# Opening loads of a two-block transformer kernel: first weight piece and transposed input in two halves, the other loads issued behind them

## The reference, cut to what matters

```
for l in range(DEPTH):                       # DEPTH = 2
    q, k, v, r, a_low, u, v_sgu = split_proj(x @ w_in[l])
    y_gla = gla_group(q, k, v, r, a_low, w_a2[l], b_a[l], gla_norm_g[l])
    y_sgu = sgu_group(u, v_sgu, w_s[l], b_s[l], sgu_ln_g[l], sgu_ln_b[l])
    h = jnp.concatenate([y_gla, y_sgu], axis=-1) @ w_out[l]
    x = layer_norm(DN_ALPHA * x + h, ...)
    x = layer_norm(DN_ALPHA * x + mem_xattn(x, mem, ...), ...)
    x = layer_norm(DN_ALPHA * x + grouped_moe(x, ...), ...)
...
# second block: its modulation vectors come from c alone
m = jax.nn.silu(c) @ w + b                   # adaln, w is 1024 x 6144, per layer
```

## Time and profile before

| | |
|---|---|
| median of three runs | 2224.72 us (2221.09 to 2226.09) |
| profiled execution, its own time | 2221.31 us |
| its span, first to last instruction | 2219.5 us |
| PE / PEld busy | 2040.2 us (92%) / 1579.8 us (71%) |
| DVE / ACT / POOL busy | 1564.4 us (70%) / 1067.9 us (48%) / 60.2 us (3%) |
| moved by DMA | 574.60 MB, 259 GB/s over the span |

### The profile page before, as it was taken

The page is one execution under the profiler, slowest core; times in us unless marked ns, Lnnn a source line. Parts: engine busy times, 40 slices in busy tenths (PEclk is TensorE's granted clock), DMA queues, the critical chain, the costliest instruction groups (busy, mean ns, idle before and its releaser), DMA issues.

```text
span 2219.5 us, 24051 instructions
## 1 busy us (share of the span) xinstructions
PE 2040.2 (92%) x9132; PEld 1579.8 (71%) x9132; DVE 1564.4 (70%) x1998; ACT 1067.9 (48%) x1090; POOL 60.2 (3%) x86
## 2 busy tenths in 40 slices
PE   7999989999799997999997988799999777899996
PEld 4566578888557575888876865588888564788885
DVE  2744479888745536888885355799989544888996
ACT  1201157777311012767762354377777332577772
POOL 0100000000000000000000000000000000000000
PEclk9999979999999997999998989799999998899998
DMA  9856169899785642989994501289889521699992
GB/s 406 335 209 279 69 232 362 336 357 361 270 360 212 235 192 85 370 320 365 370 355 153 193 35 39 110 327 350 326 330 348 181 76 46 240 351 347 355 358 112
DMA packets 49210, 574.60 MB, mean 259 GB/s; under 512 B 5056, under 2 KB 9152, under 8 KB 10688
## 3 DMA queue, kind: packets, MB, share of 16 engines
q1 hardware_dynamic: 34560, 500.19, 59.6%
q0 software_dynamic: 8352, 59.77, 6.8%
q10 hardware_dynamic: 6176, 12.97, 1.6%
HBM read 569.77 MB, written 3.15 MB: 258 GB/s over the span
## 4 chain that ended last, share of the span: by engine, by line
PE 68%; issue 17%; DVE 8%; DMA 3%; ACT 2%; POOL 0%; DVEq 0%; ACTq 0%; POOLq 0%
PE bank L767 66%; PE bank L797 2%; DVE ring_parts L1832 2%; DMA hi_ring<-in_ada 1%; DMA x<-in_x_in 1%; DVE work L1832 1%; ACT mix L1392 1%; DVE mix L1958 1%; ACT work L1392 1%; DVE hi_ring L2284 1%; DVE mix L1832 0%; DVE work_parts L1832 0%; ACT work_parts L1392 0%; DVE mix L2298 0%; DVE small L1832 0%
## 5 line engine op out<-in xcount | busy, mean ns | idle before, releaser
L1832 DVE TENSOR_TENSOR ring_parts<-ring,hi_ring_parts 128x2048 fp32r<-128x2048 f32 x398 | 894.3, 2286 | 83.7 <-ACT hi_ring_parts L1392 82.9
L1392 ACT ACTIVATE hi_ring_parts<-ring 128x2048 fp32r<-128x2048 f32 x398 | 753.5, 1914 | 219.0 <-PE bank L767 129.0
L767 PE MATMUL bank<-hi_ring_parts,tokens 128*128 128x512 f32 x2048 | 662.8, 393 | 3.1 <-DVE mix L1832 1.7
L767 PEld LDWEIGHTS bank<-hi_ring_parts,tokens 128*128 128x128 f32 x2048 | 384.6, 188 | 85.0 <-DVE mix L1832 3.3
L767 PE MATMUL bank<-ring_parts,tokens 128*128 128x512 f32 x1024 | 399.0, 390 | 0.0
L767 PE MATMUL bank<-hi_ring_parts,work_parts 128*128 128x512 f32 x1024 | 326.4, 390 | 5.7 <-DVE work_parts L1832 5.7
L1392 ACT ACTIVATE work<-bank 128x512 f32<-128x512 f32 (+6 forms) x207 | 108.6, 528 | 447.5 <-PE bank L767 434.2
L767 PEld LDWEIGHTS bank<-hi_ring_parts,work_parts 128*128 128x128 f32 x1024 | 192.2, 188 | 46.7 <-DVE work_parts L1832 6.6
L767 PEld LDWEIGHTS bank<-ring_parts,tokens 128*128 128x128 f32 x1024 | 192.6, 188 | 37.6
L767 PE MATMUL bank<-ring_parts,work_parts 128*128 128x512 f32 x512 | 199.3, 389 | 0.0
L767 PE MATMUL bank<-ring,oT 128*128 128x512 f32 x384 | 166.1, 593 | 4.7 <-DVE oT L1864 2.3
(11 more groups left out here) (210 smaller groups left out, 1871.2 us busy)
## 6 DMA issues: line engine op xcount, KB each, us to landing
ring<-in_weights SPq DMA_DIRECT2D x238, 2048.0 KB, 8.2
hi_ring<-in_ada POOLq DMA_DIRECT2D x48, 1024.0 KB, 10.6
work<-in_vecs POOLq DMA_DIRECT2D x8, 1024.0 KB, 5.1
work<-bias_rows ACTq DMA_DIRECT2D x4, 1024.0 KB, 8.5
work<-in_memT_in ACTq DMA_DIRECT2D x2, 1024.0 KB, 13.6
bias_rows<-work ACTq DMA_DIRECT2D x8, 256.0 KB, 5.9
params<-in_prm ACTq DMA_DIRECT2D x1, 1389.5 KB, 13.1
consts<-in_cst ACTq DMA_DIRECT2D x1, 1040.0 KB, 18.8
```

The source lines that it names most:

```text
L767: ins = nc.tensor.matmul(o, lhsT, rhs, start=start, stop=stop)
L1392: return nc.scalar.activation(o, i, f, **kw)
L1832: return v.tensor_tensor(o, a, b, op)
```

## The change

Four edits. SP loads p0 as two transfers of half a piece, the first raising `first_half`, the second `slot_full[0]`; and p1 waits for `slot_full[0]` instead of `xT_loaded`. ACT loads `xT` as two transfers of four chunks each (`xT_half`, `xT_loaded`), and then waits for `slot_full[0]` before it issues `params`, `consts`, `memT` and `x`. TensorE, in the first layer, begins with the first four chunks of the first half of q and of the first half of k, then waits for the second halves, and does the rest. Number and size of the matmuls stay the same.

```diff
+            def queries_and_keys(tg):
+                w = columns(ring[:, 0, :])
+                taken[0] += 1
+                owed[0] = 2
+                q_bank, k_bank = begin(f"{tg}.q"), begin(f"{tg}.k")
+                def queries(m, rows):
+                    for c in rows:
+                        ins = mm(q_bank[:, m * S:(m + 1) * S], w[:, c, m * P:(m + 1) * P], xT[:, c, :], c == 0, c == DC - 1)
+                    return ins
+
+                def keys(T, rows):
+                    for c in rows:
+                        ins = mm(k_bank[:, T * S:(T + 1) * S], xT[:, c, T * P:(T + 1) * P], w[:, c, 256:512], c == 0, c == DC - 1)
+                    return ins
+
+                pe.wait_ge(xT_half, 16)
+                pe.wait_ge(first_half, 16)
+                queries(0, range(0, 4))
+                keys(0, range(0, 4))
+                pe.wait_ge(xT_loaded, 16)
+                pe.wait_ge(slot_full[0], 16)
+                queries(0, range(4, 8))
+                end(f"{tg}.q", queries(1, range(DC)))
+                keys(0, range(4, 8))
+                ins = keys(1, range(DC))
+                end(f"{tg}.k", ins)
...
-            act.dma_start(xT[:, :, :], xT_in).then_inc(xT_loaded, 16)
+            act.dma_start(xT[:, 0:4, :], xT_in[:, 0:4, :]).then_inc(xT_half, 16)
+            act.dma_start(xT[:, 4:8, :], xT_in[:, 4:8, :]).then_inc(xT_loaded, 16)
+            act.wait_ge(slot_full[0], 16)
             act.dma_start(params[:, :], prm).then_inc(setup_loaded, 16)
...
-            for j in range(RING):
+            sp.dma_start(ring[:, 0, 0:HALF], weights[0, :, 0:HALF]).then_inc(first_half, 16)
+            sp.dma_start(ring[:, 0, HALF:PIECE], weights[0, :, HALF:PIECE]).then_inc(slot_full[0], 16)
+            for j in range(1, RING):
                 if j == 1:
-                    sp.wait_ge(xT_loaded, 16)
+                    sp.wait_ge(slot_full[0], 16)
```

More of the change, by code:

```diff
@@ L485, in program @@
         xT_loaded, mem_loaded = sem("xT_loaded"), sem("mem_loaded")
+        xT_half, first_half = sem("xT_half"), sem("first_half")
         vecs_loaded = sem("vecs_loaded")
@@ L1133, in bias_rows @@
                                                         cs("onehot")[0:33, :])])])
+            def queries_and_keys(tg):
[22 more added lines that the diff above has]
+                end(f"{tg}.k", ins)
             def first_layer(l):
+                tg = f"{l}"
                 if l == 0:
-                    pe.wait_ge(xT_loaded, 16)
+                    queries_and_keys(tg)
+                    pe.wait_ge(setup_loaded, 32)
                 else:
@@ L1140, in first_layer @@
                         ready(f"{l - 1}.turn3.{q}")
[L1141 to L1147, removed]
+                    w = columns(piece())
+                    transposed(f"{tg}.q", [lambda c, m=m: w[:, c, m * P:(m + 1) * P] for m in range(2)])
+                    product(f"{tg}.k", [(T * 256, (T + 1) * 256, P, [(xT[:, c, T * P:(T + 1) * P], w[:, c, 256:512])
+                                                                   for c in range(DC)]) for T in range(NT)])
                 wl = pr("w_alow", 2, DC * 16)[:, l, :].rearrange("p (c n) -> p c n", c=DC)
```

## The result

The new kernel takes 2232.12 us (median of 6 runs, 2229.64 to 2232.78); the old one, measured beside it, 2224.67 us. The ratio is 1.003, with an interval of 1.0019 to 1.004: 7.5 us slower by the medians. The span of its profiled execution is 2227.8 us, 8.3 more than before.

The account below looks back on a forecast made before the run. The prediction took DVE's wait for ada_w loads, set by full DMA engines, as the bound, with PE having slack. A 3.2 us hole plus 5.0 us of p7 gave +8.2 us, 2232.9 us; range 2226 to 2237.

Parts of the forecast that it names:

- the hole: After p0 and xT, from 10.0 to 13.2 us, DMA moves nothing: 3.2 us, bounds 1.2 and 4.2.
- What bounds the kernel: Before PE's restart at 96.91 us, DVE waits on ada_w loads, last a9, set by DMA bytes; PE has 3.7 us slack.
- The early start: At the kernel's start, PE begins at 7.6 us, 3.6 us earlier, without waiting for the second halves.
- p7: Weight load issued at 74.3 us; all its 2.10 MB go ahead of a9, the last ada_w load awaited: 5.0 us.
- Clock at the restart: TensorE's clock loss when PE restarts after waiting for DVE, taken as the same as before: nothing added.
- The sum's last step: From profiled execution, 2229.5 us, to median: 3.4 us added as in the old kernel, giving 2232.9.
- Only the hole counts: Rival: p7 stays behind a9, the last ada_w load awaited; +3.2 us, 2227.9; chance 0.12.
- The weights take the hole: Rival: the delay falls on p1 to p4, not waited for; a9 comes on time, 2224.7; chance 0.1.
- "warm clock" rival: TensorE's clock is full at the 105 us restart, so some 2.5 us are not paid: +5.7, 2230.4; chance 0.1.

Follow-up runs that it names:

- Experiment 4: New kernel without ACT's wait and with weight load p7 held until a9, a load of ada_w, has landed: ratio 1.0002.
- Experiment 6: Old kernel with weight loads p5, p6 and p7 held until a9, a load of ada_w, has landed: 2216.97 us, ratio 0.9966.
- experiment 1: New kernel without ACT's wait, so params, consts, memT and x are queued at once: 2228.28 us, ratio 1.002.
- experiment 3: New kernel with weight load p7 held until a9, a load of ada_w, has landed: 2226.25 us, ratio 1.0011.
- 8: New kernel, ACT's wait kept, with weight loads p5 to p7 held until a9, a load of ada_w, has landed: 2219.56 us, ratio 0.997.
- 7: New kernel without ACT's wait, with weight loads p5 to p7 held until a9, a load of ada_w, has landed: 2215.73 us, ratio 0.995.
- experiment 2: Old kernel with ACT made to wait for xT and all of p0 before issuing params, consts, memT and x: 2232.24 us, ratio 1.0041.

## Why the prediction was right, point by point

The forecast was +8.2 us, to 2232.9; measured were 2232.12, 7.5 us above the old kernel's median, and +7.85 us at the restart. Both terms of the sum and the path that they were put on are borne out, the hole with a size 0.2 to 0.7 us too large.

- *What bounds the kernel.* Right. Experiment 4 starts PE 3.7 us earlier and moves the restart by 0.4. Experiment 6 leaves PE's start alone, takes 4.2 MB from ahead of a9, and a9 is summed 6.4 us earlier.
- *The early start.* 7.6 us forecast, 7.31 measured; no gap at the second halves; 0.8 us forecast for `consts`, 0.78 measured. The second halves landed at 10.8 instead of 11.2. The missing `params` behind them are not the reason: in experiment 1, where `params` is queued at once, SP sees them at 10.88 too. v began 3.66 us early, not 2.7, because `consts` landed at 24.2 and not at 25.2, and q and k, which took 16.2 us instead of 16.8, ended at 23.5 and not at 24.4; the wait between the two came out as forecast because both were early by about as much.
- *The hole.* 3.2 us forecast, 2.5 measured by bytes. In trace time it costs 3.0 (experiment 3) and 2.7 (8 against 7). The issue at 10.83 rather than 11.2 is about half of the difference. The picture of 3.2 us "in which nothing moves" was also wrong: bytes moved again between 11 and 12 us (180 GB/s), but slowly, and the full rate was back only at 14, not at 13.2. The Trainium skill, "DMA: Bandwidth & Descriptors", "Anatomy of one DMA", gives its fixed cost of about 2.0 us for loads issued by GpSimd, while the loads at the hole are issued by ACT and SP; the hole of 2.0 us, an estimate from that figure, is below the measured 2.5.
- *p7.* 5.0 us forecast, 5.4 measured where it is alone (experiment 1), 4.8 as the difference between the new kernel and experiment 3. That the early PE alone suffices to put p7 ahead is shown by experiment 1; that a hole alone does is shown by experiment 2 for one of 3.1 us, where the prediction asked for 3.0.
- *Additivity.* The restart is late by 7.85 us, and by 5.4 and 3.0 with one cause each. The sum is 8.4, somewhat above the whole.
- *Clock at the restart.* Taken as unchanged, and nearly so: 3.78 us for `mix` in both, and 15.12 instead of 14.78 us for the keys, which is most of the 0.4 us by which the rest of the span grew. The way there was another one, see below. The row of 95 to 96 us in the earlier trace rows is the third microsecond of the wait from 93.2, not the second.
- *The sum's last step.* The 3.4 us between the profiled execution and the median are spread of the runs, not a mechanism; in the new kernel they were 2.5. That the forecast median is off by 0.8 us only is in part luck.
- *The rivals.* "Only the hole counts" would have been 2227.9; experiment 3 builds that case, and its restart is 3.0 us late. "The weights take the hole" had something in it: `x` did land where it did before, at 32.58. But the bytes not moved were missing later: a0 is summed from 52.27 instead of 48.69.

## What to carry to other kernels

Where the DMA engines are full, as here at 421 to 424 GB/s, the question for any load is not when it is issued but how many bytes stand ahead of the one that the path waits for: a wait that empties the queues costs its hole to everything behind it, and an engine that gets faster off the path asks for its next piece sooner and may push it in front of that load. Before starting an engine earlier, look whether anything waits for it; here the halves that alone cost 4.4 us are part of a kernel 10.7 us faster than the old one, once the weights and vectors not yet wanted are held behind the loads that are. A prefetch that merely becomes possible needn't be issued at once.

## What the runs showed of the hardware that I had not expected

How long TensorE's clock survives a wait differed, between kernels and between two waits of one program. In the new kernel PE's last matmul of u ends at 86.06, and the granted clock falls to 0.50 (1.2 GHz) 4.1 us later; the products of `kv`, which begin after 6.91 us of idleness, run at half clock. It is full again (2.4 GHz) from 97, stays so through 5.1 us of the second wait, from 98.65, and falls just before `mix`. (The moment of a fall is an estimate from the mean of the window in which it lies.) Windows of 1 us of the new kernel:

```profile
90.00:91.00 1.00, 0.00 (x0) 0.00 (x0) 1.00 (x3) 0.00 (x0) 0.00 (x0) 0.57 1.04 434
...
95.00:96.00 1.00, 1.00 (x4) 0.81 (x3) 0.89 (x4) 0.00 (x0) 0.00 (x0) 0.50 1.00 418
96.00:97.00 1.00, 1.00 (x4) 0.72 (x4) 0.86 (x5) 0.00 (x0) 0.00 (x0) 0.51 0.36 148
97.00:98.00 1.00, 1.00 (x6) 0.90 (x5) 0.33 (x2) 0.00 (x0) 0.55 (x1) 1.00 0.12 49
...
102.00:103.00 1.00, 0.00 (x0) 0.00 (x0) 0.96 (x2) 0.00 (x0) 0.00 (x0) 1.00 0.00 0
103.00:104.00 1.00, 0.00 (x0) 0.00 (x0) 0.97 (x2) 0.00 (x0) 0.00 (x0) 0.90 0.00 0
104.00:105.00 1.00, 0.24 (x1) 0.24 (x2) 0.97 (x2) 0.00 (x0) 0.00 (x0) 0.50 0.00 0
```

In the old kernel it fell 2.1 us into the wait. In experiment 2 it fell 5.2 us after the first wait began, when PE was already at work on `kv` again, and 2.0 us into the second wait. So the length of a wait alone does not say whether the clock is still full at its end. The "warm clock" rival of the prediction missed by about a microsecond; that an earlier restart would have kept the full clock wasn't tried.
